# GpSimd in place of VectorE for four weight subtractions per layer of a hybrid decoder trunk

## The reference

```python
h = rms_norm(x, norm_g)
proj = jnp.einsum('bsd,de->bse', h, w_in)
u_lru, u_s5, qkv_ret, q_nsa, kv_nsa, bg_nsa, gate_paths, merge = split_columns(proj, IN_SIZES)
y_lru = rg_lru_mixer(u_lru, ...)
y_s5 = s5_mixer(u_s5, ...)
y_ret = retention_mixer(...)
y_nsa = nsa_mixer(q_nsa, kv_nsa, ...)
ys = jnp.stack([y_lru, y_s5, y_ret, y_nsa], axis=2) * jax.nn.silu(gate_paths)
branch = jnp.einsum('bsnw,nwd->bsnd', ys, w_branch)
merged = jnp.sum(jax.nn.sigmoid(merge) * branch, axis=2)
return x + jnp.einsum('bsd,de->bse', merged, w_out)
```

## Time and profile before

| | before |
|---|---|
| median of 3 runs | 751.04 us (749.69 to 751.25) |
| the profiled execution, its own time | 749.62 us |
| span of the profile, first to last instruction | 747.8 us |
| PE busy | 734.8 us, 98% of the span |
| DVE busy | 486.2 us, 65% |
| ACT busy | 421.2 us, 56% |
| POOL busy | 307.4 us, 41% |
| mean granted clock of PE | 0.998 of full speed |

### The profile page before, as it was taken

The page is one execution under the profiler, slowest core; times in us unless marked ns, Lnnn a source line. Parts: engine busy times, 40 slices in busy tenths (PEclk is TensorE's granted clock), DMA queues, the critical chain, the costliest instruction groups (busy, mean ns, idle before and its releaser), DMA issues.

```text
span 747.8 us, 14583 instructions
## 1 busy us (share of the span) xinstructions
PE 734.8 (98%) x6014; PEld 623.7 (83%) x6014; DVE 486.2 (65%) x786; ACT 421.2 (56%) x676; POOL 307.4 (41%) x135
## 2 busy tenths in 40 slices
PE   8999999999999999999989999999999999999996
PEld 7888898889888888878888878988898788888785
DVE  5989977675685634535688799767565947153344
ACT  7885635538464655544558664444476345655442
POOL 3000000035977976688100000000647979766750
PEclk9999999999999999999999999999999999999999
DMA  8669637553553655555545875665625456545541
GB/s 261 188 197 272 218 124 226 185 180 114 159 151 115 196 147 144 164 173 167 150 95 169 283 190 172 202 201 187 200 85 169 134 149 175 168 137 170 172 137 56
DMA packets 87009, 126.85 MB, mean 170 GB/s; under 512 B 22072, under 2 KB 32672, under 8 KB 86944
## 3 DMA queue, kind: packets, MB, share of 16 engines
q1 hardware_dynamic: 86624, 125.63, 55.9%
q10 hardware_dynamic: 320, 0.30, 0.1%
HBM read 124.86 MB, written 1.05 MB: 168 GB/s over the span
## 4 chain that ended last, share of the span: by engine, by line
PE 93%; DVE 3%; issue 2%; ACT 1%; DMA 0%; POOL 0%; SPq 0%; POOLq 0%; DVEq 0%; ACTq 0%
PE proj L1745 68%; PE M L1740 5%; PE proj L1782 4%; PE proj L1786 2%; PE proj L1813 2%; PE M L2140 2%; PE M L1942 1%; DVE sc L1556 1%; PE M L1953 1%; PE M L1910 1%; PE proj L1828 1%; PE proj L1844 1%; PE M L2114 1%; PE M L2017 1%; PE M L2109 1%
## 5 line engine op out<-in xcount | busy, mean ns | idle before, releaser
L698 POOL TENSOR_TENSOR w_lo<-raw,w_hi 128x1024 fp32r<-128x1024 f32 x112 | 291.4, 2633 | 391.8 <-ACT w_hi L720 368.7
L720 ACT ACTIVATE w_hi<-raw 128x1024 fp32r<-128x1024 f32 x200 | 206.5, 1054 | 108.8 <-PE proj L1745 64.8
L1745 PE MATMUL proj<-w_hi,h_hi 128*128 128x512 f32 x544 | 216.8, 399 | 0.0
L1745 PE MATMUL proj<-w_hi,h_lo 128*128 128x512 f32 x544 | 212.4, 390 | 0.0
L1745 PE MATMUL proj<-w_lo,h_hi 128*128 128x512 f32 x544 | 212.0, 390 | 0.0
L1745 PEld LDWEIGHTS proj<-w_hi,h_lo 128*128 128x128 f32 x544 | 102.1, 188 | 22.2 <-issue 0.5
L1745 PEld LDWEIGHTS proj<-w_hi,h_hi 128*128 128x128 f32 x544 | 102.2, 188 | 21.8 <-issue 0.9
L1745 PEld LDWEIGHTS proj<-w_lo,h_hi 128*128 128x128 f32 x544 | 102.3, 188 | 20.4 <-issue 0.5
L1329 DVE TENSOR_TENSOR w_lo<-raw,w_hi 128x1024 fp32r<-128x1024 f32 x80 | 95.0, 1221 | 27.0 <-ACT w_hi L720 19.5
L1745 PE MATMUL proj<-w_hi,ys_hi 128*128 128x512 f32 x128 | 51.0, 398 | 0.0
L1745 PE MATMUL proj<-w_hi,ys_lo 128*128 128x512 f32 x128 | 50.0, 391 | 0.0
(11 more groups left out here) (342 smaller groups left out, 1175.7 us busy)
## 6 DMA issues: line engine op xcount, KB each, us to landing
raw<-in_w_in SPq DMA_DIRECT2D x152, 512.0 KB, 4.3
raw<-in_w_branch SPq DMA_DIRECT2D x32, 512.0 KB, 4.0
raw<-in_w_out SPq DMA_DIRECT2D x16, 512.0 KB, 4.1
raw<-in_s_w_glu SPq DMA_DIRECT2D x8, 512.0 KB, 4.8
raw<-in_w_in SPq DMA_DIRECT2D x8, 256.0 KB, 3.0
merged<-in_nsa_ck_w SPq DMA_DIRECT2D x4, 512.0 KB, 6.9
mt<-in_nsa_ck_w SPq DMA_DIRECT2D x4, 512.0 KB, 8.9
merged<-in_nsa_cv_w SPq DMA_DIRECT2D x4, 512.0 KB, 4.6
```

Source lines behind the costliest of these rows:

```text
L698: nc.gpsimd.tensor_tensor(w_lo[:, slot(s, l), 0:n * w], raw[:, u % N_RAW, 0:n * w], w_hi[:, slot(s, l), 0:n * w].bitcast(f32), ALU.subtrac ...
L720: i = nc.scalar.activation(out_, in_, func, **kw)
L1745: last = mm(dst, left[i], right[j], start=start and n == 0, stop=stop and n == 2, skip_group_check=True)
```

## The change

The four low halves of `nsa_kv` in each layer move from DVE to POOL: the name leaves `LO_ON_VECTOR`, the two calls of `split_lo` leave DVE's list, and the two counts for a layer follow (44 to 40 for DVE, 56 to 60 for POOL).

```diff
-LO_ON_VECTOR = ("u_s5", "ret_v", "nsa_kv", "gate_s5", "gate_lru", ...
+LO_ON_VECTOR = ("u_s5", "ret_v", "gate_s5", "gate_lru", ...
...
-    "lam_abs": 1, "lam_exp": 1, "lo_done": 56, ...
+    "lam_abs": 1, "lam_exp": 1, "lo_done": 60, ...
...
-    "vk_ready": 2, "vlo_done": 44, ...
+    "vk_ready": 2, "vlo_done": 40, ...
...
                     scan_steps(0)
-                    split_lo("nsa_kv", 0, 1)
                     scan_out(0)
-                    split_lo("nsa_kv", 2, 3)
                     angles(1)
```

More of the change, by code:

```diff
@@ L73 @@
 SPLIT_UNITS = [u for u in range(NU) if CHUNKS[UNITS[u][0]][0] not in NATIVE]
-LO_ON_VECTOR = ("u_s5", "ret_v", "nsa_kv", "gate_s5", "gate_lru", "merge_s5_0", "merge_s5_1", "ret_q", "ret_k", "nsa_q",
+LO_ON_VECTOR = ("u_s5", "ret_v", "gate_s5", "gate_lru", "merge_s5_0", "merge_s5_1", "ret_q", "ret_k", "nsa_q",
                 "out_0b", "out_1b")
@@ L108 @@
     "hid_tm_ready": 2, "hlo_done": 8, "kcT_done": 1, "kcT_ready": 1, "kc_ready": 1, "kern_ready": 2, "kp_done": 2,
-    "lam_abs": 1, "lam_exp": 1, "lo_done": 56, "lru_act": 16, "lru_m2": 1, "lru_mm": 1, "lru_sqrt": 1,
+    "lam_abs": 1, "lam_exp": 1, "lo_done": 60, "lru_act": 16, "lru_m2": 1, "lru_mm": 1, "lru_sqrt": 1,
     "mT_done": 2, "mag_arg": 1, "mag_exp": 1, "mhi_done": 2, "mlo_done": 2, "mt_free": 6, "nT_done": 2,
@@ L115 @@
     "v0_ready": 1, "v_ready": 2, "var": 2, "vbd_ready": 1, "vecT": 2, "vec_ready": 1, "vectors_loaded": 208,
-    "vk_ready": 2, "vlo_done": 44, "wT_done": 4, "wT_ready": 4, "w_ready": 2, "wbd_ready": 2, "wl_loaded": 64,
+    "vk_ready": 2, "vlo_done": 40, "wT_done": 4, "wT_ready": 4, "w_ready": 2, "wbd_ready": 2, "wl_loaded": 64,
     "xT_done": 4, "x_half": 3, "x_scaled": 4, "xc_ready": 1, "y_done": 2, "y_ready": 2, "yg_hi": 4, "yg_lo": 4,
```

## The result

| | before | after |
|---|---|---|
| median of 20 runs | 749.72 us (749.17 to 751.60, and one run of 1902.22) | 751.79 us (750.38 to 754.89) |
| ratio to before, 95% interval | | 1.0027 [1.0018, 1.0036] |
| span of the profile | 747.8 us | 753.1 us |

The change makes the kernel slower by 2.0 us (1.4 to 2.7). I had forecast 1.05 us. The profiled execution of after is the slowest of its runs: PE was 2.70 us late before it came to anything that the change touches. It began `gate_s5` at 86.26 us; in before that was 83.56. The rest is the clock: the 16 products behind that wait took 3.62 us, where before's took 2.15, and the granted clock was 0.50 from 15 to 17 us. I therefore subtract 2.70 us from times of this profile when I compare them with before.

The account below looks back on a forecast made before the run. PE, busy for 98% of the span, was taken to bound the kernel. PE waits of 0.65 (first layer) and 0.3 (second) plus 0.1 for restarts, 1.05 us, on 751.04 gave 752.1 us; own range 751.4 to 753.3, full range 750.7 to 754.8.

Parts of the forecast that it names:

- slower by over 0.2%: Outcome for the whole kernel: time more than 0.2%, about 1.5 us, above before; chance 0.38.
- the same time: Outcome for the whole kernel: time within about 0.2%, 1.5 us, of before; chance 0.59.
- The turns: POOL low halves and two-SBUF-input DVE steps alternate, 2.26 and 0.54 us; L1260 3.3 us late, `trig(1)` 2.3 us late.
- The deadlines of the first layer: PE's needed inputs: `nsa_kv` and start of `gate_s5` covered; at `own_outputs(1)` PE stands 0.65 us.
- DVE gets the first turns: Rival: DVE keeps the lock through L1302 to L1305; PE waits 1.5 us a layer at `nsa_kv`'s second unit; 754.1 us, chance 0.14.
- The second layer's 0.3 us: `keep_kernels(1)` ends at 461.5 instead of 459.21, PE wants it at 461.19, so PE waits 0.3 us.
- the tenth for restarts: Term of the sum: one more tenth of a microsecond for two restarts of PE.
- I cost this at nothing: The four `gate_s5` loads wait for POOL; the last starts 0.9 us later, its high half still in time: no cost.
- more lateness: Rival: one more microsecond of DVE lateness, say from `gate_s5` loads, costs PE one in each layer; 754.1 us, chance 0.15.

Follow-up runs that it names:

- the kernel whose POOL only writes: Against the changed kernel, POOL fills the four low halves of `nsa_kv` with zeros by memsets instead of subtracting: 750.97 us, ratio 1.0022.
- the second profile: The changed kernel run and profiled once more, nothing edited: 752.03 us, ratio 1.0027, span 748.9.
- the load held: Against the changed kernel, in the second layer SP issues the third load of `gate_s5` only when `state_inputs(1)` is done: 750.87 us, ratio 1.0015.
- `own_outputs(1)` moved: Against the changed kernel, PE takes `own_outputs(1)` behind the fourth unit of `gate_s5` instead of the third: 750.57 us, ratio 1.0012.

## Why the prediction was right, and where it was wrong

The direction and the range held. That the time itself lies 0.3 us from the forecast's 752.1 is luck: before's median was 749.72 in 20 runs and not the 751.04 of three, and the loss was larger than forecast by nearly as much. Against before the change cost 2.0 us where the sum had 1.05, at the upper end of the forecast's own 0.4 to 2.3 (751.4 to 753.3 less 751.04). It came out slower by 0.27%, which I had given 0.38 (slower by over 0.2%) against 0.59 for the same time; the interval, from 0.18% on, does not quite shut out the latter. By the steps, times of after less 2.70:

- **The turns** came as worked out: 2.26 us for POOL, 0.54 for DVE. L1304 ends at 72.14 (forecast 72.03), L1260 starts at 73.96 (73.85), L1266 ends at 79.13 (79.09), ACT's `trig(1)` starts at 79.16 (79.13). The sentence of the Trainium skill's "SBUF — State Buffer" that I cited there (section "Who interferes with whom") says that the reading of both engines is what excludes them; the kernel whose POOL only writes agrees, with 0.68 us for the two-input DVE instructions inside a fill. One reading of the code was off without effect: L1263, like L1266, has one input, and POOL had ended before either.
- **The deadlines of the first layer**: the copies of `nsa_kv` end at 83.32 (forecast 83.4), and `gate_s5` starts without a wait. The second unit of `nsa_kv` was in time, so the rival "DVE gets the first turns" did not happen. `keep_kernels(1)` ends at 94.64 (94.58), and PE stands for 0.68 us, 0.5 in the second profile (forecast 0.65). **Right.**
- **The second layer's 0.3 us**: DVE's part is right. In the second profile of after `keep_kernels(1)` ends at 461.51, the 461.5 of the forecast. PE did not wait for it, because PE was by then 1.1 us late for another reason. The term came as a wait in no profile, not even with the load held, and the tenth for restarts has no row of its own.
- **The step that failed** is the one on the four loads of `gate_s5`: "I cost this at nothing". I had asked only whether the weights of these loads come in time, and they do. I took the last load's 0.9 us of delay for all there was, and did not ask what the third, which goes out earlier than in before (435.71 against 436.35), meets on its way. It meets PE's instructions, for 0.9 us of idle PE in one profile and 1.8 in the other.

What the measured 2.0 us consist of: the second profile of after, free of the late start, has 0.48 and 0.93 us, 1.4 together. The mean granted clock of each run, which the record has, says where more comes from. Among the runs at 0.998 or above, the medians are 750.89 and 750.74 us for after (first 20 runs, and once more) and 749.45 to 749.55 for before (in its three later series): 1.2 to 1.4 us apart, as the profile has it. Runs at 0.997 or less have 752.38 and 752.62 in after, 750.58 to 751.21 in before, and they are 15 of 29 in after but 24 of 83 in before. So some 0.6 of the 2.0 us is that the clock fell in more of its runs, an estimate from these medians. In one profile, that of the kernel whose POOL only writes, such a fall came behind the gap; whether the gap brings them on no run shows. With `own_outputs(1)` moved, the runs at 0.998 or above have 750.36, 0.4 to 0.5 below after, which fits the wait of 0.5 to 0.7 us; by the ratios of all runs the two kernels are 1.1 us apart.

So the forecast's sum was too small by the second loss and by the clock, for which it had no term. The rival "more lateness" had named the loads of `gate_s5` as a possible source, but thought of late weights and a late `gate_s5`, and its loss of 3.05 us was 1 us too large.

Shown: the turns need POOL's reading; the wait at `own_outputs(1)` is their price; the gap comes and goes with the timing of one load, and comes in before too when a load is put there. Inferred: that the q8 transfers are PE's instructions (by their number, and by PE going on 2.2 to 2.8 us after the start of each one that comes late), and that they queue behind the packets of a load. Open: why the gap of the same kernel was 1.3 us once and 2.2 us once, why the clock fell in more runs of after, and why the gap has no like in the first layer. There the transfer behind `state_inputs(1)` starts at 72.70 in before, so that the batches end at another place in the program; I have not tried to shift them.

## What to carry to other kernels

Time taken off an engine that nobody waits for is worth nothing, and the one that takes it over may hold it up for more than it took: price a GpSimd instruction that reads SBUF, beside VectorE instructions with two inputs in SBUF, at the whole of its length. When a change moves the moment at which a large load is issued, ask not only whether its data come in time, but what else must pass the DMA engines in that microsecond, above all where TensorE runs through many small products. A gap of PE put down to "issue", with all its operands there, is the sign of that. And when such a gap is mended, look whether the next one shows.

## What the runs showed of the hardware that I had not expected

- PE's program comes, as its 47 transfers let me infer, in pieces of 16 KB, one for 256 instructions, and PE goes on 2.2 to 2.8 us after the start of the one it waits for (11 profiles). A stretch of 128 small products and 128 loads uses a batch up in 1.8 us.
- A load of 512 KB at the wrong moment delayed such a transfer by up to 1.8 us, and moving one load by 3.5 us (434.98 for 431.52) made the kernel 1.35 us slower.
- GpSimd's fills of SBUF left the two-input instructions of VectorE that ran beside them at 0.68 us; beside its subtractions such took 2.31 to 2.88. VectorE's one-input instructions of 0.43 us took 0.54 and 0.71 beside the fills.
- Nearly the same idle time of PE, 1.80 and 1.82 us, was followed once by a granted clock of 0.50 for some 3 us and once by none. In a wait of 8.2 us the clock fell before PE went on.
